# State-space scan: a pair's two y products, once one burst per head, now alternating piece by piece in one burst per pair

## The reference, cut to what matters

```
cb = jnp.einsum('bclgn,bcsgn->bgcls', c_c, b_c)
y_diag = jnp.einsum('bgcls,bgecls,bcsgep->bclgep', cb, decay_in, xdt)
...
y = (y_diag + y_off).reshape(b, nc * Q, SSM_D_INNER)[:, pf:pf + L]
y = y + (xs.reshape(b, L, SSM_HEADS, P).astype(f32) * d_skip.astype(f32)[:, None]).reshape(b, L, SSM_D_INNER)
hg = (y * jax.nn.silu(z.astype(f32))).reshape(b, L, G, SSM_D_INNER // G)
hg = hg * lax.rsqrt(jnp.mean(hg * hg, axis=-1, keepdims=True) + NORM_EPS)
hg = hg.reshape(b, L, SSM_D_INNER) * gate_g.astype(f32)
return hg.astype(u.dtype) @ w_out
```

## Time and profile before

| | |
|---|---|
| median of three runs | 3166.29 us (3163.63 to 3168.21) |
| span of the profiled execution | 3159.4 us |
| outside the span, median less span | 6.9 us |
| TensorE busy over the span | 97% |
| first y product starts | 274.94 us |
| first output tile inside the loop starts | 349.60 us |
| last y product ends | 486.1 us |

### The profile page before, as it was taken

How to read it: one execution, slowest core, us unless ns; L and a number is a source line. 1 busy time by engine, 2 the same in 40 slices (tenths; PEclk the granted TensorE clock), 3 DMA queues, 4 the chain that set the end, 5 groups by cost and what they waited for, 6 DMA issues and landing times.

```text
span 3159.4 us, 48143 instructions
## 1 busy us (share of the span) xinstructions
PE 3079.1 (97%) x18576; PEld 2645.8 (84%) x18576; DVE 1907.7 (60%) x2663; ACT 1146.9 (36%) x1976; POOL 531.5 (17%) x537
## 2 busy tenths in 40 slices
PE   8999999999999999999999999999999999999998
PEld 8997779999998888989886667888887677788886
DVE  7855666857564555857576556444579757654444
ACT  4234443322243665422233334222333453432223
POOL 4400213400011333410000001000035233200001
PEclk9999999999999999999999999999999999999999
DMA  3221012222222101222232222222222100022222
GB/s 131 93 87 34 16 35 76 89 88 92 87 101 67 35 34 44 97 93 87 94 100 80 74 67 80 94 93 93 95 94 90 60 1 1 21 94 93 93 94 86
DMA packets 64933, 235.72 MB, mean 75 GB/s; under 512 B 7312, under 2 KB 7312, under 8 KB 64784
## 3 DMA queue, kind: packets, MB, share of 16 engines
q1 hardware_dynamic: 63504, 229.44, 21.8%
q0 software_dynamic: 1280, 4.20, 0.4%
HBM read 231.51 MB, written 2.10 MB: 74 GB/s over the span
## 4 chain that ended last, share of the span: by engine, by line
PE 83%; DVE 10%; issue 4%; ACT 2%; DVEq 0%; POOL 0%; DMA 0%; SPq 0%; ACTq 0%; POOLq 0%
PE ps L274 44%; PE ps L303 21%; DVE conv_acc L350 3%; PE ps L800 2%; PE ps L2015 1%; PE ps L2022 1%; PE ps L1280 1%; PE ps L1241 1%; PE ps L1640 1%; PE ps L1668 1%; PE ps L1266 1%; PE ps L1260 1%; DVE conv_in L337 1%; DVE w_low L233 1%; DVE conv_acc L347 1%
## 5 line engine op out<-in xcount | busy, mean ns | idle before, releaser
L274 PE MATMUL ps<-x_hi,w_high 128*128 128x264 f32 (+2 forms) x2712 | 705.8, 318 | 17.6 <-DVE x_lo L369 12.4
L274 PE MATMUL ps<-x_lo,w_high 128*128 128x264 f32 (+2 forms) x2712 | 702.6, 317 | 0.0
L274 PE MATMUL ps<-x_hi,w_low 128*128 128x264 f32 (+2 forms) x2712 | 700.8, 317 | 0.0
L228 ACT ACTIVATE w_high<-w_raw 128x1024 fp32r<-128x1024 f32 x426 | 446.6, 1049 | 424.3 <-DMA w_raw<-in_slabs 423.9
L233 DVE TENSOR_TENSOR w_low<-w_raw,w_high 128x1024 fp32r<-128x1024 f32 x346 | 438.3, 1267 | 193.0 <-ACT w_high L228 192.8
L274 PEld LDWEIGHTS ps<-x_hi,w_high 128*128 128x128 f32 x2712 | 448.8, 189 | 60.7 <-issue 12.0
L274 PEld LDWEIGHTS ps<-x_lo,w_high 128*128 128x128 f32 x2712 | 448.1, 189 | 34.1 <-issue 1.0
L274 PEld LDWEIGHTS ps<-x_hi,w_low 128*128 128x128 f32 x2712 | 448.7, 190 | 33.3
L350 DVE SCALAR_TENSOR_TENSOR conv_acc<-conv_in,par,conv_acc 128x528 f32<-128x528 f32 (+1 forms) x320 | 374.3, 1170 | 46.7 <-DVE conv_acc L347 3.7
L446 POOL TENSOR_TENSOR sqa<-sqa,rvar 128x512 f32<-128x512 f32 (+2 forms) x31 | 41.9, 1352 | 1364.1 <-ACT rvar L438 1362.8
L380 DVE TENSOR_TENSOR h<-ps,h 128x512 f32<-128x512 f32 (+1 forms) x120 | 83.2, 693 | 288.7 <-PE ps L274 201.3
(11 more groups left out here) (415 smaller groups left out, 4731.2 us busy)
## 6 DMA issues: line engine op xcount, KB each, us to landing
w_raw<-in_slabs SPq DMA_DIRECT2D x426, 512.0 KB, 3.5
rel_bias<-in_rel POOLq DMA_DIRECT2D x16, 256.0 KB, 2.9
h<-in_x SPq DMA_DIRECT2D x4, 528.0 KB, 7.1
out_y<-h SPq DMA_DIRECT2D x8, 256.0 KB, 2.1
consts<-in_consts SPq DMA_DIRECT2D x1, 968.0 KB, 10.5
consts<-in_consts SPq DMA_DIRECT2D x1, 448.0 KB, 4.1
par<-in_params SPq DMA_DIRECT2D x1, 346.5 KB, 4.1
```

The lines of the kernel that those rows point to most:

```text
L228: act.activation(w_high[:, n % RING, :], w_raw[:, n % RING, :], ACT.Copy).then_inc(S("w_hi"), 1)
L274: mm = pe.matmul(ps[:, 2 * tslot + k, 0:n], w, a[:, kb, c:c + n], start=first, stop=fin)
```

## The change

The single `y_product(hh)` after every head becomes `y_products(p)` after every odd head. It waits for the weights of both heads, then goes through the seven pieces and issues each piece for the even head and at once for the odd head. The semaphore `ssd_y` rises by two at the end instead of by one after each head. Nothing else is edited.

```diff
-            def y_product(hh):
-                p, po, e, g = hh // 2, 64 * (hh % 2), hh % HPG, hh // HPG
-                if hh % 2 == 0 and p:
+            def y_products(p):
+
+                g = 2 * p // HPG
+                if p:
                     pe.wait_ge(S("ssd_y_taken"), p)
-                if e == 0:
+                if 2 * p % HPG == 0:
                     pe.wait_ge(S("ssd_xt_taken"), 3 * g + 3)
-                pe.wait_ge(S("ssd_m"), hh + 1)
+                pe.wait_ge(S("ssd_m"), 2 * p + 2)
                 for i, (s0, n, _) in enumerate(LBLK):
                     for bk, c, t, m in PIECES[i]:
-                        mm = pe.matmul(ps[po:po + 64, Y_BANK + bk, c:c + m], x_tok[0:n, g % 2, i, 64 * e:64 * e + 64],
-                                       dec[0:n, hh % 3, packed(i, t):packed(i, t) + m], start=i == 0,
-                                       stop=(bk, i) in ((0, 1), (1, 4)), skip_group_check=True)
-                mm.then_inc(S("ssd_y"), 1)
+                        for z in range(2):
+                            hh = 2 * p + z
+                            e = hh % HPG
+                            mm = pe.matmul(ps[64 * z:64 * z + 64, Y_BANK + bk, c:c + m],
+                                           x_tok[0:n, g % 2, i, 64 * e:64 * e + 64],
+                                           dec[0:n, hh % 3, packed(i, t):packed(i, t) + m], start=i == 0,
+                                           stop=(bk, i) in ((0, 1), (1, 4)), skip_group_check=True)
+                mm.then_inc(S("ssd_y"), 2)
...
-                y_product(hh)
+                if hh % 2:
+                    y_products(hh // 2)
```

## The result

The changed kernel takes 3178.31 us (3178.03 to 3179.57), before 3166.29 us (3163.63 to 3168.21): ratio 1.0041, 95% interval 1.0028 to 1.0053, from five executions of each. I had forecast 3153.6 and at most 3172. It is 12 us slower, on the side to which I had given 0.22.

The account below looks back on a forecast made before the run. TensorE was taken to set the pace. First half -15.6 and second half +2.9 gave -12.7 us, from 3166.3 to 3153.6 us (-0.4%); own range 3147 to 3161, with partial overlap 3147 to 3172.

Parts of the forecast that it names:

- the side to which I had given 0.22: Whole kernel: slower than before, 0.22, made of 0.19 from no overlap and 0.03 from partial overlap.
- What bounds the kernel: Whole span and scan: TensorE sets the pace, busy for 97% of the span, with its clock granted in full.
- The burst: Products of two heads: side by side in separate column halves, 2.70 us per pair instead of 5.26, saving 41.0 us.
- the -4 that I wrote: Whole kernel: sum near -4 us if three column tiles' efficiency of 0.79 held, a pair then taking 3.3 us.
- First half, -15.6: Heads 0 to 13: 17.9 us saved by overlap, 2.0 of PSUM waits gone, 4.3 of new waits: -15.6 us.
- one wait that I put at 1.2 us: After burst 6, end of first half: transposes wait for evictions, 1.2 us more than before.
- Second half, +2.9: Scan with output tiles: 23.0 us saved, 26.4 of new waits, 0.5 of old waits gone: +2.9 us.
- waits for add_out: Second half: even output tile must be added before its slot is free; new waits sum to 26.4 us.
- One mechanism could add more: TensorE's clock drops behind long waits, some 1.7 us each; part of a rival on miscounted waits, inside the forecast's range.
- The chain: Behind each burst: decay and weights, in the second half also slab_hi, slab_lo, add_out; 4.4 us first half, 8.3 second.
- No overlap: Rival at the burst: columns run one after the other, 5.2 to 5.26 us; 3192 to 3194 us, chance 0.19.

Follow-up runs that it names:

- the control: The kernel before with the 128-row broadcasts alone, one product per head kept in its old place: 3160.4 us, ratio 0.9987.

## Why the prediction was wrong

- *What bounds the kernel*: right for before. That it stays TensorE, at its full clock, was assumed but for one rival.
- *The burst*: right. I took 2.70 us from two matmuls in separate rows, and it is 2.64. The estimate from the three column tiles of the Trainium skill, "TensorE: Matmul & The Clock Gate", Part 3, was 3.3 us. (With it my sum comes to -12.7 + 16 x 0.61 = -3 us, not to the -4 that I wrote.) The measurement decides: two column tiles of float32 gave 1.98 of 2. The rule in the same part of the Trainium skill that loads overlap with matmuls in flight only when the row group differs does not bite either; the 28 loads, all of one row group, passed beside the matmuls.
- *First half, -15.6*: with the clock held it is -13.2; 2.3 of the rest are one wait that I put at 1.2 us. In the changed kernel it was -7.0. What the sum left out is the low clock, which comes with the move: it puts two 32-row broadcasts side by side, where a y product stood between them.
- *Second half, +2.9*: with the clock held it is +1.6. The waits for add_out were 23.3, not 26.4 us. In the changed kernel it was +22.4, of which some 4 are the low stretch that the wait of step 13 leaves behind.
- *The step that failed* is in the rivals: "One mechanism could add more", a lowered clock behind a wait, put "inside the forecast's own range" at some 1.7 us a time, for waits near 4.9 us. The runs showed it behind shorter waits too, and where nearly none was, thirteen times in the scan by the trace's clock. Priced as I priced it, the rows of the changed kernel miss 66.8 x 0.14 + 161.9 x 0.18 = 38.5 us of full clock, 3.0 a time and not 1.7. How much of that reached the span the control tells. The clock is 27 of the 28 us: the scan is 15.4 us longer than before in the changed kernel, and 198.6 - 210.2 = 11.6 us shorter than its control's in the kernel with filled waits and wide broadcasts. The chain, the burst and the order of size of the waits were right; this was a rival that deserved a sum and a sign of its own. Numbers that I had pointed to it: TensorE was to be idle for some 30 of 200 us, and to do 41 us less of 128-row work. How often the clock would fall, they did not say.
- *No overlap*, to which I gave nearly all of the slow side's 0.22, was wrong. That the time came out on its side is no merit of it.

Not settled is how broadcasts, short waits and bursts share in the first half's low clock. Wide broadcasts removed it but for the stretch behind the wait of 3.5 us, but I did not try the moved products without two neighbouring narrow broadcasts, and single falls came in the old order too. Nor was a fourth `dec` buffer tried, which would let ScalarE run on ahead of the burst.

## What to carry to other kernels

When an edit takes work off TensorE without taking the time off the others, sum what TensorE does per stretch and treat a lowered clock as a rival with its own price: here 27 us against a gain of 12. Two narrow float32 products that write different column halves are worth pairing, but see what else had run in the time of the one that moves. And a stall moves: look which queue has the item that everyone waits for behind work that nobody does; here one rounding moved ahead of the exponentials and one tile moved behind the burst turned +0.4% into -0.4%, and into -0.95% together with the wide broadcasts.

## What the runs showed of the hardware

Two float32 matmul streams in the array's columns 0 to 63 and 64 to 127, same rows and same PSUM banks, take 2.64 us instead of 5.23. TensorE's clock fell to 1.2 GHz at us 275.9 and 303.2 with no wait over 0.6 us beside it, where six of the eight matmuls in each of two neighbouring broadcasts used 32 rows; the same matmuls over 128 rows, zeros in 96 of them, kept the clock at 0.98 for 59.1 us, where it had been 0.86 for 66.8. Behind the same instructions and a wait of 0.7 us it fell in one run and held in another. Where the clock was full already, a broadcast over 128 rows still took 1.49 us instead of 1.59. Matmuls without a use, put into waits, made the kernel 17.6 us faster.
